# A hybrid state-space, attention and expert network on one core: the time-step projection computed with its weights stationary beside the first chunk, and the soft-plus chain cut into pieces

## The chip, the core and the metric

The kernel runs on one core of a Trainium2 chip. The engines are TensorE (PE), VectorE (DVE), ScalarE (ACT), GpSimd (POOL) and SyncE (SP), and 16 DMA engines move data. Each engine runs its own list of instructions in order and waits on semaphores. The metric is the time of one execution in device microseconds, as a median of several runs. All data is float32 unless marked otherwise. In the traces a float32 matmul appears as two records.

## What is computed

Two layers over 256 latent tokens and 256 context tokens, 512 in all, of width 1024. Layer 0 mixes tokens with a bidirectional state-space scan (SSD), layer 1 with local attention; each is followed by a mixture of 16 experts. Every part starts with a normalisation whose scale and shift come from a conditioning vector c through a large matrix ada_w. The change touches the start of layer 0:

```python
sh1, sc1, g1, sh2, sc2, g2 = split(silu(c) @ ada_w[l] + ada_b[l])
a_l = modulate(rmsnorm(h, norm1_w[l]), sh1, sc1)        # x * (1 + scale) + shift

def project(h):                                          # in ssd_mixer
    zxbcdt = h @ in_w
    z = zxbcdt[..., :D_INNER]
    xbc = silu(centred_dwconv(zxbcdt[..., D_INNER:D_INNER + CONV_DIM], conv_w, conv_b))
    dt_raw = zxbcdt[..., D_INNER + CONV_DIM:]            # 64 columns: 32 heads, two directions
    dt_f = softplus(dt_raw[..., :SSM_HEADS] + dt_bias[0])
    dt_b = softplus(dt_raw[..., SSM_HEADS:] + dt_bias[1])
    return z, xs, bm, cm, dt_f, dt_b

cum = cumsum(dt_c * a_neg, axis=2)                       # in ssd_chunked_scan, per block of 128 tokens
```

## The kernel before

Tokens lie along the columns: hT holds x and aT the normalised input, each as 8 tiles of 128 features by 512 tokens (k from 0 to 7). The order of work is written out by hand for each engine, and semaphores tie the engines together. The opening of the kernel runs like this.

**Loads.** SP issues the DMAs: a slice of constants, x, ctx, erev, nine small loads of packed parameters (packs), then the weight units in the order of the list `order`: ada0 to ada7 (1 MB each, a piece of ada_w), xbc0 (1 MB, two chunks of ssd_in_w as 1024 packets of 1 KB), ada8, ada9, xbc1, and so on. A unit whose slot holds an earlier unit waits until PE is done with that one. ACT issues on its own queue, at the very start: wdtw (the 64 columns of ssd_in_w that give dt_raw, 128x8x64), the router's weights rw, and five rows broadcast over all partitions (dtb, expa, dskip, rb, sink). After the first modulations ACT also issues the rest of the constants, c32 and c16.

**Turning x and the squares.** PE turns x (L1106), with the packed parameters in front of the last piece (L1102). DVE and ACT copy the pieces to hT. ACT squares each tile into aT (L786). PE computes four ada units (L1117: four 32-column tiles of 512 columns each, summed in one bank), then the mean square as eight 512-column matmuls over the squares (L1136), then ada4 to ada7, and turns the resulting rows (ada_turn, L1130).

**Normalisation.** ACT takes the square root (L788), DVE the reciprocal (L1864), then DVE multiplies the eight tiles (L1869); before tile 3 it copies the ada rows (L1832), and before tile 6 it forms shift and scale (L1838, L1846). ACT modulates each tile in two halves (L795).

**Time-step projection.** For each tile k, four matmuls with 128 tokens of aT as stationary weights and the 64 columns of wdtw[k] as moving operand (L1161), so that tokens come out on the partitions. Then a chain on DVE (L1876 to L1894) with one Exp on ACT (L812) computes the soft-plus as a series, dt, and dt times the decay rate (sp[6]).

**Chunks.** in_chunk(i) is eight matmuls of 512 columns (L1174). ACT copies the result with padding (conv_in, L832), DVE convolves in five steps (L1931, L1934), ACT takes Tanh (L839), DVE finishes the SiLU (L1945). Each of the first 14 chunks is followed on PE by one ada unit. After chunk 6 PE forms cumulative sums from sp[6] with triangular matrices (L1291 to L1294). From chunk 14 on, chunks alternate with the scan itself. Later come the gate z, the output projection, the experts (L1491, L1530), attention and the second set of experts, with weights streamed through a ring of slots by SP.

`link` on DVE makes an instruction wait for the one before it. `add_squares(i, k, n)` already existed for the later normalisations: it adds the squares of tile k to ssq. `mean_square_of_sum` multiplies ssq and the last tile's squares with the constant matrix mean.

## Time and profile before

| what | value |
|---|---|
| median of 3 runs | 1526.36 us (1525.91 to 1527.06) |
| the profiled execution | 1528.73 us, of which the span of the trace is 1526.9 us |
| PE busy | 1404.9 us (92%), weight loads 795.6 us |
| DVE busy | 543.7 us (36%) |
| ACT busy | 393.5 us (26%) |
| POOL busy | 152.1 us (10%) |
| mean granted PE clock | 0.968 of full speed |
| DMA | 334.46 MB, mean 219 GB/s |
| chain of waits that ended last | PE 70%, issue on SP 13%, DMA 6%, DVE 5%, ACT 2% |

The span runs from the first to the last instruction; some 1.8 us lie outside it. A share of busy time is an average over stages with different limits, so what a change in one stage is worth is read from that stage. Line numbers in the rows are those of the kernel before.

### The profile page before, as it was taken

To read this page: it belongs to the slowest core of one execution; us is meant where nothing else is said; L and a number is where in the kernel's file an instruction comes from. 1 tells how busy PE (TensorE), PEld (TensorE's weight loads), DVE (VectorE), ACT (ScalarE), POOL (GpSimd) and SP (SyncE) were. 2 spreads that over 40 slices of the span, in tenths; PEclk is the share of its full clock that TensorE was granted. 3 is DMA by queue.
4 is the path that set the end of the run, shared out by engine and by line. 5 is a ranking of instruction groups with operands and counts; after the bars stand their busy time and mean duration, and the time that the engine had idled before them with its cause. 6 is when DMAs were issued, how large, how long until landed. Compare 5 with 4: busy or idle time off the path is not lost.

```text
span 1526.9 us, 28680 instructions
## 1 busy us (share of the span) xinstructions
PE 1404.9 (92%) x12237; PEld 795.6 (52%) x12237; DVE 543.7 (36%) x1010; ACT 393.5 (26%) x961; POOL 152.1 (10%) x181
## 2 busy tenths in 40 slices
PE   5899899999988999989999999998999999989876
PEld 2534444454544444455566555646856775555432
DVE  2445656555553221144122221124254442221112
ACT  2321333334434310040222222204053302221111
POOL 0000113122042200000011111000000001111100
PEclk9799999999999999999999999999999999999988
DMA  9365333344341452152999999993330359999993
GB/s 354 112 216 174 131 111 135 117 138 164 110 138 57 110 138 83 57 195 74 364 356 389 392 382 381 360 362 105 112 111 2 127 195 392 394 392 400 398 404 133
DMA packets 131493, 334.46 MB, mean 219 GB/s; under 512 B 13283, under 2 KB 63259, under 8 KB 125211
## 3 DMA queue, kind: packets, MB, share of 16 engines
q1 hardware_dynamic: 118763, 307.56, 55.2%
q0 software_dynamic: 6208, 12.60, 2.4%
q10 hardware_dynamic: 6384, 12.36, 2.2%
q8 instruction: 100, 1.64, 0.4%
q14 instruction: 38, 0.31, 0.1%
HBM read 325.79 MB, written 14.81 MB: 223 GB/s over the span
## 4 chain that ended last, share of the span: by engine, by line
PE 70%; SPq 13%; DMA 6%; DVE 5%; ACT 2%; issue 2%; DVEq 0%; ACTq 0%; POOLq 0%
PE ps L1174 11%; PE ps L1491 10%; SPq L557 10%; PE ps L1387 7%; PE ps L1191 7%; PE ps L1530 5%; PE ps L1441 5%; SPq L559 3%; PE ps L1117 3%; PE ps L1791 2%; PE ps L1555 2%; PE ps L1703 2%; PE ps L1266 2%; DMA ring<-in_moe_w_down 1%; PE ps L1279 1%
## 5 line engine op out<-in xcount | busy, mean ns | idle before, releaser
L1174 PE MATMUL ps<-aT,ring 128*128 128x512 f32 x384 | 174.6, 604 | 0.0
L1491 PE MATMUL ps<-ring,ssb 128*32 128x256 f32 x2256 | 132.2, 386 | 13.3 <-DMA ring<-in_moe_w_up 12.6
L1491 PE MATMUL ps<-tmp,ssb 128*32 128x256 f32 x1984 | 113.0, 380 | 10.0 <-DMA tmp<-in_moe_w_up 10.0
L2214 DVE COPY big<-ps 32x256 f32<-32x256 f32 x162 | 68.6, 424 | 146.0 <-PE ps L1530 144.3
L1174 PEld LDWEIGHTS ps<-aT,ring 128*128 128x128 f32 x384 | 71.4, 193 | 82.8 <-issue 82.8
L1191 PE MATMUL ps<-aT,ring 128*128 128x512 f32 x256 | 114.2, 595 | 0.0
L2205 DVE TENSOR_TENSOR ssb<-ssb,ps 128x128 f32<-128x128 f32 (+1 forms) x56 | 19.4, 348 | 257.4 <-ACT ssb L968 257.4
L1387 PE MATMUL ps<-big,ring 128*128 128x512 f32 x256 | 110.2, 592 | 0.0
L1491 PEld LDWEIGHTS ps<-ring,ssb 128*32 128x32 f32 x2256 | 74.0, 111 | 65.9 <-DMA ring<-in_moe_w_up 19.7
L1530 PE MATMUL ps<-ring,ssb 128*32 128x256 f32 x1648 | 96.8, 387 | 3.5 <-DMA ring<-in_moe_w_down 2.9
L871 ACT ACTIVATE ssb<-ps,dt 128x128 f32<-128x128 f32 x256 | 73.3, 372 | 88.5 <-PE ps L1254 87.7
L981 ACT COPY big<-ps 32x256 f32<-32x256 f32 x162 | 58.7, 362 | 141.4 <-PE ps L1530 139.9
L1491 PEld LDWEIGHTS ps<-tmp,ssb 128*32 128x32 f32 x1984 | 66.6, 110 | 53.1 <-DMA tmp<-in_moe_w_up 9.5
L1441 PE MATMUL ps<-aT,ring 128*128 128x256 f32 (+1 forms) x288 | 89.3, 468 | 4.4 <-ACT aT L795 4.4
L968 ACT ACTIVATE ssb<-ps 128x128 f32<-128x128 f32 (+1 forms) x56 | 18.2, 325 | 257.3 <-PE ps L1491 257.2
L1387 PEld LDWEIGHTS ps<-big,ring 128*128 128x128 f32 x256 | 48.6, 190 | 61.2 <-issue 61.0
L1191 PEld LDWEIGHTS ps<-aT,ring 128*128 128x128 f32 x256 | 47.2, 190 | 52.6 <-issue 52.6
L1934 DVE SCALAR_TENSOR_TENSOR ring<-ring,par 128x512 f32<-128x512 f32 x96 | 72.2, 752 | 3.4
L1441 PEld LDWEIGHTS ps<-aT,ring 128*128 128x128 f32 x288 | 55.0, 196 | 35.2 <-issue 29.3
L1530 PEld LDWEIGHTS ps<-ring,ssb 128*32 128x32 f32 x1648 | 52.8, 111 | 38.7 <-issue 5.2
L746 POOL DMA_INDIRECT y_rows<-big,sidx x32 | 30.1, 940 | 315.7 <-DVE big L2214 314.3
L786 ACT ACTIVATE aT<-hT 128x512 f32<-128x512 f32 (+1 forms) x32 | 17.7, 574 | 159.8 <-DVE hT L2076 88.5
(393 smaller groups left out, 1828.6 us busy)
## 6 DMA issues: line engine op xcount, KB each, us to landing
ring<-in_ada_w SPq DMA_DIRECT2D x44, 1024.0 KB, 4.9
ring<-in_moe_w_down SPq DMA_DIRECT2D x40, 1024.0 KB, 17.9
ring<-in_moe_w_gate SPq DMA_DIRECT2D x56, 512.0 KB, 11.6
ring<-in_moe_w_up SPq DMA_DIRECT2D x56, 512.0 KB, 15.7
tmp<-in_moe_w_gate SPq DMA_DIRECT2D x48, 512.0 KB, 12.9
tmp<-in_moe_w_up SPq DMA_DIRECT2D x48, 512.0 KB, 16.4
ring<-in_ssd_in_w SPq DMA_DIRECT2D x20, 1024.0 KB, 7.4
tmp<-in_moe_w_down SPq DMA_DIRECT2D x16, 1024.0 KB, 17.6
```

What stands on the lines that cost most here:

```text
L557: sp_.dma_start(pair_slot(u)[:, :, r, :], src).then_inc(s_w[u.slot], 16)
L559: sp_.dma_start(slot(u, 2), down[(j - 4) * 2 * P:(j - 3) * 2 * P, :].rearrange("(k p) n -> p k n", p=P))\
L871: ins = act.activation(E[:, d * HG + h, :], ps[:, 5, j * P:(j + 1) * P], ACT.Exp, bias=dt[:, t, col:col + 1])
L981: ins = act.copy(Y[s % 2][32 * g:32 * g + 32, 256 * c:256 * c + 256], tiled_y[32 * c:32 * c + 32, 2 * h + i, :])
L1174: ins = pe.matmul(ps[:, bank, :], slot(u)[:, k, (i % 2) * P:(i % 2 + 1) * P], aT[:, k, :], start=(k == 0), stop=(k == KD - 1))
L1191: ins = pe.matmul(ps[:, z_bank(i), :], slot(u)[:, k, (i % 2) * P:(i % 2 + 1) * P], aT[:, k, :], start=(k == 0), stop=(k == KD - 1))
L1387: ins = pe.matmul(ps[:, 4 + m % 4, :], w[:, k, :], xT[:, k, :], start=(k == 0), stop=(k == KI - 1))
L1441: ins = pe.matmul(ps[:, 2 * (f % 2) + r, per * h:per * h + per], pair_slot(unit(e, k // 2))[:, k % 2, r, f * P:(f + 1) * P], aT[:, k, per ...
L1491: ins = pe.matmul(tiled_gu[32 * c:32 * c + 32, 2 * h + i, :].rearrange("p (r n) -> p r n", r=2), XgT[l][:, k * C + 32 * g:k * C + 32 * g + ...
L1530: ins = pe.matmul(tiled_y[32 * c:32 * c + 32, 2 * h + i, :], hiddenT[l][:, g, 32 * k:32 * k + 32], slot(units["x", l, s, 4 + k // 2][0], 2 ...
L1934: ins = dve.scalar_tensor_tensor(out=o, in0=pre[i % 2][:, :, tap:tap + S], scalar=par[:, tap * NCONV + ch:tap * NCONV + ch + 1], in1=o, op ...
L2214: ins = dve.tensor_copy(Y[s % 2][32 * g:32 * g + 32, 256 * c:256 * c + 256], tiled_y[32 * c:32 * c + 32, 2 * h + i, :])
```

## The change

1. **Mean square.** DVE adds the squares of tiles 0 to 6 into ssq as ACT produces them (add_squares for k = 1 to 6). PE computes five ada units, then two matmuls, over ssq and over the last tile's squares, in place of eight, then three more ada units. The shared counter s_ssq starts one higher for later users. In the normalisation the ada rows are copied before tile 4 and not 3, shift and scale are formed before tile 7 and not 6.
2. **Projection.** wdtw[k] (128x64) is now stationary and aT[k] (512 columns) moves. Even k write partitions 0 to 63 of PSUM bank 4, odd k partitions 64 to 127. PE takes tiles in pairs: the first chunk's two matmuls for k and k + 1, then the two projection matmuls (dt_parts). DVE copies the bank to dtT. After chunk 1 and its ada unit, PE multiplies the four token blocks of dtT with `two` (two identities on top of each other), which adds the two halves and puts tokens on partitions (dt_sums). POOL builds `two`.
3. **Soft-plus.** The DVE chain is cut into four pieces, which run behind the convolutions and SiLUs of chunks 1 to 4. ACT's Exp, the exponential of the decay rates and the copies of dskip move behind the first Tanh and the second conv_in; its Ln moves from chunk 4 to 5.
4. **Loads.** All loads are issued by SP. Ada0 stands before the packed parameters; behind xbc0 follow wdtw and the rows dtb, expa and dskip; behind ada8, ada9 and xbc1 follow c32, c16 and erev; rw, rb and sink come after four more units. ACT begins with a Silu of one element.

```diff
-        n_consts, n_x, n_bc = 10, 3, 5
+        n_consts, n_late, n_x, n_bc, n_rt = 9, 3, 3, 4, 3
...
-            sp_.dma_start(erev[:, :], a["erev"]).then_inc(s_const, 16)
...
-            for name, v in order:
+            load(*order[0])
+            for i, r, src in packed:
+                sp_.dma_start(packs[r:r + src.shape[0], i, :], src).then_inc(s_const, 16)
+            for name, v in order[1:KD + 1]:
                 load(name, v)
+            sp_.dma_start(wdtw, a["ssd_in_w"][0][:, DI + NCONV * P:DI + NCONV * P + 64].rearrange("(k p) n -> p k n", p=P))\
+                .then_inc(s_bc, 16)
+            for dst, src in ((dtb[:, :], a["ssd_dt_bias"].rearrange("l d h -> (l d h)")),
+                             (expa[:, :], a["ssd_a_log"].rearrange("l d h -> (l d h)")),
+                             (dskip[:, :], a["ssd_d"].rearrange("l h -> (l h)"))):
+                sp_.dma_start(dst, src.partition_broadcast(P)).then_inc(s_bc, 16)
+            for name, v in order[KD + 1:KD + 4]:
+                load(name, v)
...
+            pool.wait_ge(s_x, 16 * n_x)
+            pool.tensor_tensor(two, ident[:, 0:HP], ident[:, HP:P], ALU.add).then_inc(s_set, 1)
...
+            act.activation(small[:, 14:15], small[:, 15:16], ACT.Silu)
...
+                if i == 1:
+                    act.wait_ge(s_sp, 5)
+                    act.activation(sp[1], sp[1], ACT.Exp, scale=-1.0).then_inc(s_sp, 1)
+                    act.wait_ge(s_bc, 16 * n_bc)
+                    act.activation(expa[:, :], expa[:, :], ACT.Exp).then_inc(s_sp, 1)
...
-            for n in range(4):
+            for n in range(5):
                 ada_unit(n)
-            mean_square(0, T, 7)
-            for n in range(4, KD):
+            mean_square_of_sum(0, T, 7, 1)
+            for n in range(5, KD):
                 ada_unit(n)
             ada_turn(0)
-
-
-            pe.wait_ge(s_bc, 16 * 7)
-            for k in range(KD):
-                pe.wait_ge(s_a, k + 1)
-                for t in range(NT):
-                    ins = pe.matmul(ps[:, 4, t * 64:(t + 1) * 64], aT[:, k, t * P:(t + 1) * P], wdtw[:, k, :],
-                                    start=(k == 0 and t == 0), stop=(k == KD - 1), skip_group_check=True)
-            ins.then_inc(s_sp, 1)
...
+            def dt_parts(k):
+                for r in range(k, k + 2):
+                    ins = pe.matmul(ps[HP * (r % 2):HP * (r % 2) + HP, 4, :], wdtw[:, r, :], aT[:, r, :],
+                                    start=(r < 2), stop=(r >= KD - 2))
+                return ins
+
+            def dt_sums():
+                pe.wait_ge(s_sp, 2)
+                pe.wait_ge(s_set, 10)
+                for t in range(NT):
+                    ins = pe.matmul(ps[:, 6, t * 64:(t + 1) * 64], dtT[:, t * P:(t + 1) * P], two, start=True, stop=True)
+                ins.then_inc(s_sp, 1)
+
+            pe.wait_ge(s_bc, 16 * n_bc)
+            for k in range(0, KD, 2):
+                for r in range(k, k + 2):
+                    pe.wait_ge(s_a, r + 1)
+                    in_chunk(0, r, r + 1)
+                ins = dt_parts(k)
+            ins.then_inc(s_sp, 1)
...
             for i in range(AHEAD):
-                in_chunk(i)
+                if i:
+                    in_chunk(i)
                 ada_unit(KD + i)
+                if i == 1:
+                    dt_sums()
...
-            norm(0, T, {3: ada_rows, 6: modulation})
+            for k in range(1, KD - 1):
+                add_squares(0, k, T)
+            norm(0, T, {4: ada_rows, 7: modulation})
...
+                if 1 <= i <= 4:
+                    softplus(i - 1)
```

PE, from the first ada unit on. In these names ring, ssb and tmp are the slots that hold weight units, cs is the conditioning vector, aT the squares and later the input, and ssb in the projection is wdtw. Before:

```order
L1117 MATMUL ps<-ring,cs 32x512 x16
L1136 MATMUL ps<-aT,mean 128x512 x8
L1117 MATMUL ps<-ssb,cs 32x512 x8
L1117 MATMUL ps<-tmp,cs 32x512 x8
L1130 MATMUL ps<-c,ring 128x128 x4
L1161 MATMUL ps<-ssb,aT 128x64 x32
L1174 MATMUL ps<-aT,ring 128x512 x8
L1117 MATMUL ps<-ring,cs 32x512 x4
L1174 MATMUL ps<-aT,ring 128x512 x8
L1117 MATMUL ps<-ring,cs 32x512 x4
```

Now, the same place:

```order
L1128 MATMUL ps<-ring,cs 32x512 x16
L1128 MATMUL ps<-ssb,cs 32x512 x4
L1152 MATMUL ps<-ssq,mean 128x512
L1154 MATMUL ps<-aT,mean 128x512
L1128 MATMUL ps<-ssb,cs 32x512 x4
L1128 MATMUL ps<-tmp,cs 32x512 x8
L1141 MATMUL ps<-c,ring 128x128 x4
L1176 MATMUL ps<-aT,ring 128x512 x2
L1287 MATMUL ps<-aT,ssb 64x512 x2
```

Five ada units stand ahead of a mean square of two matmuls, and the projection has gone into the first chunk in pairs of 64-wide matmuls; the last two rows come four times in all. A little further on, from the last pair to chunk 2, PE now has:

```order
L1287 MATMUL ps<-aT,ssb 64x512 x2
L1128 MATMUL ps<-ring,cs 32x512 x4
L1176 MATMUL ps<-aT,ring 128x512 x8
L1128 MATMUL ps<-ring,cs 32x512 x4
L1295 MATMUL ps<-ncum,ssb 128x64 x4
L1176 MATMUL ps<-aT,ring 128x512 x8
```

The four 64-column matmuls over ssb (dtT) and ncum (`two`) stand between chunk 1's ada unit and chunk 2.

SP's loads, before, from ada4 on (ring<-in_ssd_in_w 128x8x256 is an xbc unit):

```order
L535 DMA ssb<-in_ada_w 128x2048 x2
L535 DMA tmp<-in_ada_w 128x2048 x2
L535 DMA ring<-in_ssd_in_w 128x8x256
L535 DMA ring<-in_ada_w 128x2048 x2
L535 DMA ring<-in_ssd_in_w 128x8x256
L535 DMA ring<-in_ada_w 128x2048 x2
```

Now, the same place:

```order
L533 DMA tmp<-in_ada_w 128x2048 x2
L533 DMA ring<-in_ssd_in_w 128x8x256
L637 DMA ssb<-in_ssd_in_w 128x8x64
L642 DMA dtb<-in_ssd_dt_bias 128x64
L642 DMA expa<-in_ssd_a_log 128x64
L642 DMA dskip<-in_ssd_d 128x32
L533 DMA ring<-in_ada_w 128x2048 x2
L533 DMA ring<-in_ssd_in_w 128x8x256
L645 DMA c<-in_c 128x896
```

The load of wdtw (ssb) and three rows have come between xbc0 and ada8, and c32 (c), c16 (big) and erev behind xbc1.

## Rows read from the trace of the kernel before

**Rows 1.** Busy time by stretches; columns: us, engines, PEclk, DMA share, GB/s.
```profile
0.00:44.00 44.00, 23.96 (x124) 11.66 (x124) 12.70 (x19) 13.30 (x22) 1.01 (x13) 0.92 0.92 351
...
66.00:240.00 174.00, 164.69 (x684) 75.04 (x677) 101.22 (x153) 51.41 (x118) 11.21 (x10) 0.97 0.45 152
```
**Rows 2.** Timeline of PE; start us, length us, line, operation, what ended idle time.
```profile
9.73 4.83 PE L1106 MATMUL ps<-c,big 128*128 128x128 f32 x28 [9.73 <-DMA big<-in_ctx]
...
20.82 1.06 PE L1117 MATMUL ps<-ring,cs 128*32 128x512 f32 x8 [1.41 <-DMA ring<-in_ada_w]
...
23.30 1.93 PE L1117 MATMUL ps<-ring,cs 128*32 128x512 f32 x8 [1.41 <-DMA ring<-in_ada_w]
...
25.16 7.84 PE L1136 MATMUL ps<-aT,mean 128*128 128x512 f32 x16
...
39.77 0.69 PE L1130 MATMUL ps<-c,ring 128*128 128x128 f32 x4 [3.20 <-DVE ring L1832]
...
43.10 13.88 PE L1161 MATMUL ps<-ssb,aT 128*128 128x64 f32 x64 [2.64 <-ACT aT L795]
...
56.78 9.06 PE L1174 MATMUL ps<-aT,ring 128*128 128x512 f32 x16
...
65.77 1.07 PE L1117 MATMUL ps<-ring,cs 128*32 128x512 f32 x8
...
66.76 7.13 PE L1174 MATMUL ps<-aT,ring 128*128 128x512 f32 x16
```
**Rows 3.** Busy time by stretches, around the falls of PE's clock.
```profile
23.30:26.70 3.40, 3.40 (x10) 1.03 (x11) 0.00 (x0) 0.00 (x0) 0.00 (x0) 0.51 1.01 422
...
43.10:57.00 13.90, 13.90 (x65) 13.90 (x66) 0.00 (x0) 8.02 (x15) 1.39 (x1) 0.50 0.25 94
...
57.00:60.40 3.40, 3.40 (x5) 1.33 (x6) 2.72 (x5) 0.87 (x4) 0.00 (x0) 0.50 0.00 0
```
**Rows 4.** Timeline of DVE.
```profile
33.83 3.35 DVE L1864 RECIPROCAL rstd<-rstd 128x512 f32<-128x512 f32 x1 [17.68 <-ACT rstd L788]
...
37.22 1.90 DVE L1869 TENSOR_TENSOR aT<-hT,rstd 128x512 f32<-128x512 f32 x3
...
62.15 3.19 DVE L1888 SCALAR_TENSOR_TENSOR ssb<-ssb 128x256 f32<-128x256 f32 x7
...
82.62 0.55 DVE L1931 TENSOR_SCALAR ring<-ring,par 128x512 f32<-128x512 f32 x1 [3.76 <-ACT ring L832]
```
**Rows 5.** Timeline of ACT.
```profile
16.91 4.26 ACT L786 ACTIVATE aT<-hT 128x512 f32<-128x512 f32 x8
...
41.87 2.56 ACT L795 ACTIVATE aT<-aT,mod,amod 128x256 f32<-128x256 f32 x5 [8.14 <-DVE amod L1846]
```
**Rows 6.** Stretch from 10 to 11 us, and ACT's DMA queue in the first 20.
```profile
10.00:11.00 1.00, 1.00 (x6) 1.00 (x6) 0.12 (x1) 0.00 (x0) 0.00 (x0) 1.00 0.33 57
...
q10 hardware_dynamic: 2800, 0.43, 12.7%
```
**Rows 7.** Issues on SP's and ACT's queues; of the last two, median us to landing.
```profile
18.34 0.38 SPq L535 DMA_DIRECT2D ring<-in_ssd_in_w  x1
...
21.95 7.53 SPq L535 DMA_DIRECT2D ring<-in_ada_w  x1
...
3.02 1.10 ACTq L771 DMA_DIRECT2D expa<-in_ssd_a_log  x1
...
dtb<-in_ssd_dt_bias ACTq DMA_DIRECT2D x1, 32.0 KB, 10.0
...
c<-in_c SPq DMA_DIRECT2D x1, 64.0 KB, 2.0
```
**Rows 8.** Timeline of PE, small matmuls at full clock.
```profile
115.12 0.41 PE L1291 MATMUL ps<-ssb,c 128*128 128x32 f32 x2
...
229.68 1.09 PE L1279 MATMUL ps<-ssb 128*64 128x128 f32 x16 [0.60 <-issue]
```
**Rows 9.** Waits of SP's DMA issues: us in total, times, longest.
```profile
SPq L535 <- PE ps L1117: 380.9, 40, 36.1
```

More of the change, by code:

```diff
@@ L302, in build @@
         four = ncum[:, 0, 0:NE]
+        two = ncum[:, 0, :]
         ps = ctx.enter_context(nc.psum_tensor("ps", [P, 8, 512], F32))
@@ L526, in _ @@
                       (2, 48, a["c_ctx"].rearrange("(c p) -> c p", p=P))]
-            for i, r, src in packed:
-                sp_.dma_start(packs[r:r + src.shape[0], i, :], src).then_inc(s_const, 16)
             held = {}
@@ L632, in moe @@
                     after(l, following, False)
-            for name, v in order:
+            load(*order[0])
[10 more added lines that the diff above has]
+            for name, v in order[KD + 1:KD + 4]:
+                load(name, v)
+            sp_.dma_start(c32[:, P:], a["c32"][:, P:]).then_inc(s_const, 16)
+            sp_.dma_start(c16f, a["c16"]).then_inc(s_const, 16)
+            sp_.dma_start(erev[:, :], a["erev"]).then_inc(s_const, 16)
+            for name, v in order[KD + 4:2 * KD]:
+                load(name, v)
+            sp_.dma_start(rw[:, :, :], a["router_w"].rearrange("(k p) n -> p k n", p=P)).then_inc(s_bc, 16)
+            for dst, src in ((rb[:, :], a["router_bias"]), (sink[:, :], a["attn_sink"].rearrange("l h -> (l h)"))):
+                sp_.dma_start(dst, src.partition_broadcast(P)).then_inc(s_bc, 16)
+            for name, v in order[2 * KD:]:
                 load(name, v)
@@ L762, in _ @@
         def _(act):
-            act.dma_start(wdtw, a["ssd_in_w"][0][:, DI + NCONV * P:DI + NCONV * P + 64].rearrange("(k p) n -> p k n", p=P))\
-                .then_inc(s_bc, 16)
-            act.dma_start(rw[:, :, :], a["router_w"].rearrange("(k p) n -> p k n", p=P)).then_inc(s_bc, 16)
-            rows = [(dtb[:, :], a["ssd_dt_bias"].rearrange("l d h -> (l d h)")),
-                    (expa[:, :], a["ssd_a_log"].rearrange("l d h -> (l d h)")),
-                    (dskip[:, :], a["ssd_d"].rearrange("l h -> (l h)")),
-                    (rb[:, :], a["router_bias"]), (sink[:, :], a["attn_sink"].rearrange("l h -> (l h)"))]
-            for dst, src in rows:
-                act.dma_start(dst, src.partition_broadcast(P)).then_inc(s_bc, 16)
             act.wait_ge(s_set, 4)
+            act.activation(small[:, 14:15], small[:, 15:16], ACT.Silu)
             for k in range(1, KD, 2):
@@ L797, in norm_modulate @@
                         ins.then_inc(s_a, 1)
-                if i == 0:
-                    act.dma_start(c32[:, P:], a["c32"][:, P:]).then_inc(s_const, 16)
-                    act.dma_start(c16f, a["c16"]).then_inc(s_const, 16)
             def ready0(k):
@@ L808, in _ @@
             norm_modulate(0, 0, T, 7, ready0)
-            act.wait_ge(s_sp, 3)
-            act.activation(sp[1], sp[1], ACT.Exp, scale=-1.0).then_inc(s_sp, 1)
-            act.wait_ge(s_bc, 16 * 7)
-            act.activation(expa[:, :], expa[:, :], ACT.Exp).then_inc(s_sp, 1)
-            for w in range(2):
-                act.copy(dcol[w * HP:(w + 1) * HP, :].unsqueeze(2),
-                         dskip[w * HP:(w + 1) * HP, :].rearrange("p (k w) -> p k w", w=2)[:, :, w:w + 1]).then_inc(s_dcol, 1)
             def decays():
@@ L908, in _ @@
                 conv_in(i)
-                if i == 4:
-                    act.wait_ge(s_sp, 6)
+                if i == 1:
[3 more added lines that the diff above has]
+                    act.activation(expa[:, :], expa[:, :], ACT.Exp).then_inc(s_sp, 1)
+                    for w in range(2):
+                        act.copy(dcol[w * HP:(w + 1) * HP, :].unsqueeze(2),
+                                 dskip[w * HP:(w + 1) * HP, :].rearrange("p (k w) -> p k w", w=2)[:, :, w:w + 1]).then_inc(s_dcol, 1)
+                if i == 5:
+                    act.wait_ge(s_sp, 8)
                     act.activation(lnd, dt[:, :, :].rearrange("p t n -> p (t n)"), ACT.Ln).then_inc(s_ln, 1)
@@ L1307, in _ @@
                     turn_x(i - 2)
[L1309 removed]
+            pe.wait_ge(s_set, 11)
             pe.wait_ge(s_cT, 3)
@@ L1869, in norm @@
                         dve.tensor_tensor(aT[:, k, part], hT[:, k, part], rstd[:, part], ALU.mult).then_inc(s_nx, 1)
[L1871 to L1874 removed]
+            for k in range(1, KD - 1):
+                add_squares(0, k, T)
+            norm(0, T, {4: ada_rows, 7: modulation})
+            dve.wait_ge(s_bc, 16 * n_bc)
             dve.wait_ge(s_sp, 1)
[L1876 to L1877 removed]
```

89 lines of the change are left out of this document (50 added, 39 removed).

## The prediction, made before the change was run

> **What bounds the kernel now.** I read the table by stretches first. After the opening 44 us, TensorE (PE) is busy 164.69 of the next 174 us, so from there on PE's own work sets the pace; in the opening 44 us it is busy only 24 [rows 1]. The opening is therefore where time can come out, and what comes out ahead of the long PE run moves all that stands behind it.
>
> PE's timeline of that opening gives the chain [rows 2]. It waits for x and ctx (9.73), turns x, waits 1.41 us each for the weight units ada2 (20.82) and ada3 (23.30), sums squares from 25.16, waits for ada_rows (39.77), waits for the first modulated tile (43.10), computes the time-step projection in 13.88 us, and starts the first chunk at 56.78; the next ada unit starts at 65.77. Between the sum of squares and 43.10 the chain runs through ScalarE (ACT) and VectorE (DVE): Sqrt when the sum is done at 33.0, reciprocal of 3.35 us at 33.83, norm products of 0.63 each, modulation from 41.87 [rows 4, 5].
>
> The granted clock is the third view. It was 0.51 from 23.3 to 26.7, after the two waits for weights; 0.50 throughout the projection, after PE had been idle around ada_turn; still 0.50 in the first 3.4 us of the chunk; then it rose [rows 3]. So the projection ran wholly at the lower level (1.2 GHz) and did not lift it, while chunk matmuls of 512 columns did.
>
> **Sum of squares (removes eight matmuls from the chain).** Before: from 25.16 for 7.84 us, to 33.0, and ada4 stood behind it [rows 2]. Now DVE adds the squares and PE needs two matmuls. When can these start? ACT's squares begin at 16.91 and take 0.53 each [rows 5]; DVE's six adds, each at the 0.63 us of a 512-column product [rows 4] and some 0.1 of waiting for the one before, start after the second square and end 4.4 us later, near 22.4. The loads can come earlier: all that the ACT queue carried, 2800 small packets, had used 12.7% of 20 us, 2.5 us of all engines, in competition with x [rows 6]; this leaves the front, and so does erev. Also ada0 is now in line directly behind ctx, where the rate had fallen to 57 GB/s after 10 us [rows 6]. I put x 1.6 us earlier, so the adds end at 20.8; the units gain the 2.5 us and one more from the hole, 3.5 in all. Units land 2.48 us apart (20.82, 23.30), so ada4, now ahead of the mean square, would have landed at 25.8 and lands at 22.3. That is later than the adds, and sets the start. Warm prices: a unit of four 32-column tiles 0.99 (65.77 to 66.76), a 512-column matmul 7.1/8 = 0.89 [rows 2]. Work 0.99 + 2 x 0.89 = 2.8; at half clock for 3.4 us, as before, 1.7 of it is done, the other 1.1 follow: end at 22.3 + 3.4 + 1.1 = 26.8, **6.2 us earlier** than 33.0. Bounds: warm and ada4 at 21.5 gives 24.3; ada4 gaining only 1.5 us gives 28.8.
>
> The preloaded Silu table takes two table loads out of ACT's start, but ada4's landing, not ACT's squares, sets the mean square in this sum: nothing, and up to the 1.3 us of a load if that landing should come sooner.
>
> **The norm chain.** Reciprocal and products are as before, but four products instead of three stand ahead of ada_rows and seven instead of six ahead of the modulation: one product more, 0.63 [rows 4]. So the first modulation moves from 41.87 to 41.87 - 6.2 + 0.6 = 36.3; ada5 to ada7 (the last lands at 33.2 - 3.5 = 29.7) are done before ada_rows is wanted at 33.5. PE's first input, 1.2 us after that, is there at 37.5 instead of 43.10, **5.6 us earlier**.
>
> **Parameter loads past the projection's start.** wdtw and three broadcast rows now sit on SP's queue behind the 1024-packet xbc0. Before, the issue right behind xbc0 (18.34) took 7.53 us, until 29.48 [rows 7]. Taking 3.5 us off, SP is free for wdtw at 26; wdtw has as many packets as xbc0, so the first row waits again, until xbc0 is nearly in, near 31.5 (29.7 for ada7 plus 2.5, less a little). Three rows at 1.10 each [rows 7] make 34.8, and with the 2.0 us that a small load took to land on a queue still empty [rows 7] they land at 36.8: just ahead of 37.5. I take it as hidden, with no more than a microsecond to spare. Xbc0 itself (32.2) is in time. Units ada8 and on are issued behind the rows at 35, and not wanted before 50. The later loads (c32, c16, erev, router rows) are six more issues, 0.4 to 1.1 us each, on an engine that spends 380.9 us waiting for PE [rows 9]: nothing.
>
> **Projection and first chunk.** Removed: 13.88 us at half clock, 32 matmuls of 0.434, thus 0.217 warm and 6.9 in all. Its weight loads were busy 13.9 of 13.9 us [rows 3], so each 128x128 load of aT cost as much as its 64 columns. Added: eight matmuls of 512 columns in four pairs on separate column halves. No row shows such a pair at 512 columns. If the two overlap fully it is 0.89, if not at all 1.78. Nearest: eight 64-wide matmuls of 128 columns took 1.09 [rows 8], 0.27 a pair, where columns alone make 0.22 for one and 0.44 for two; and four 32-wide ones took 0.99 for 0.89. I take 0.97, so 3.9 for four pairs. Chunk plus pairs: 7.1 + 3.9 = 11.0 warm. From 37.5 with the clock low for 3.4 us as in [rows 3]: 1.7 done, 9.3 left, end 37.5 + 3.4 + 9.3 = **50.2 instead of 65.77**, 15.6 us earlier. ACT's modulations take 1.0 a tile (two halves of 0.51) and end near 44.5, ahead of a half-clock PE.
>
> What the row shows first: 32 matmuls of 64 columns filled 13.88 us, and their weight loads filled it too. The Trainium skill, TensorEngine Tiling (Array Packing), Performance Considerations, says that a matmul of one column costs what one of 60 does, so that 64 columns would be paid by columns. By columns alone the old projection streams 32 x 64 = 2048 of them, as much as four pairs of 512, 7.1 us at half clock; whoever costed it so would take 6.8 us less for this change and arrive at 1518.5. The measured row decides against that.
>
> Added on PE as well: dt_sums, four matmuls of 64 columns with 128x128 weights. Bounds: the old ones at 0.217, the first of the triangular matmuls (32 columns, two records) at 0.41 with its end [rows 8]; so 0.9 to 1.6, and I take 0.9, since the old ones have this very shape. **Net: 15.6 - 0.9 = 14.7.**
>
> **Soft-plus in pieces.** Off PE's path before, too: the chain ran beside the chunk. In each 8.06 us of chunk and ada unit DVE was idle 3.76 [rows 4]. The largest piece, part 2, is seven steps of 3.19 and one of 0.3: it fits. The first piece, 1.2, comes behind conv(1) and silu(0), and ACT's Exp waits for it, with conv_tanh(1) queued behind; silu(1) comes two chunks before its buffer is wanted. The cumulative sums want the result after chunk 6, some 20 us later. Nothing. Were DVE's idle time not there, the four pieces would cost their own length, some 9 us. DVE's copy of the products (0.6) has chunk 1 to hide in, ahead of dt_sums; POOL's new add of two slices of the identity runs after x has come, when POOL does nothing else, and its cast of c16 is wanted only behind 160 us.
>
> **To the end.** SP's loads wait for PE's own progress, 380.9 us in 40 waits on PE's ada units [rows 9], so the streams shift with it. The profiled span of 1526.9 becomes 1512.2; the profiled run's 1528.7 becomes 1514.0; against the median of 1526.4: **1511.7 us**.
>
> **Rivals.**
> - *The clock stays low through the mixed chunk,* as it did through the projection. Against: chunk matmuls lifted it in 3.4 us. Then 22.0 us from 37.5 end at 59.5; gain 6.3 - 0.9 = 5.4: 1521. Chance 0.06.
> - *The rows hold the projection up by some microseconds.* At four more, 1516; at seven, 1519. Chance 0.12.
> - *Given back later:* PE waits for DVE and ACT around 180 to 240 us, or a differently falling clock, eat what came in. Nothing in that stretch is tied to absolute time, but each fall of the clock is worth some 2 us (the first chunk's 9.06 against 7.1); six such would be needed. 1524 to 1529. Chance 0.07.
> - *Slower, by one queue.* If each of the small loads blocks as ada8's did: wdtw to 26, then 7.5 each for dtb, expa and dskip, 48.5, and they land, as dtb did on the busy queue [rows 7], 10 us later, 58.5. Then chunk and pairs end at 58.5 + 12.7 = 71.2, plus 0.9: 6.3 us slower, 1532.7. It decides once rows land after 52.2 (64.9 less 12.7). The Trainium skill, DMA: Bandwidth & Descriptors, Queues, rings and completion order, has each issuing engine's transfers consumed in order of its own ring, so the small ones would stand behind the big ones; the 7.53 us row agrees with that much. For it also: the margin is thin. Against: after xbc0 nothing large is left in line. Chance 0.05.
> - *The change does not reach its aim:* ada4 is late, so the mean square gains only 3; all else as told: 1515. Within the forecast.
> - *The forecast,* with the clock up all along (rows in at 36.8, + 11.0 = 47.8; gain 17.1: 1509) to half-overlapped pairs (1.4 lost), a late ada4 (2.0) and a clock low twice as long (1.7), gain 9.6: 1517. Chance 0.70.
>
> **How the numbers follow.** Low end: 1507, the warm case with rows and units 2 us earlier. High end: 1519, which takes in most of the second rival, with the first, the give-back and the slower case outside. A difference under 0.2% (3 us) can't be told from none. Faster: 0.70 + 0.06 + 0.12 = 0.88; within 0.2%: 0.07; slower: 0.05.
>
> **What would show it.** Right: Sqrt near 27, first modulation near 36, PE's chunk beginning within 1 us of it, pairs of about 1.0, ada8's matmuls near 50 and a PE without a gap to about 162. Wrong: a PE waiting for loads of dtb, expa or dskip; a clock of 0.5 past 41; pairs of 1.8; a gap in front of dt_sums or chunk 2; gaps growing behind 160 us.

## The result, and the profile of the changed kernel

The changed kernel took 1507.65 us (median of 4 runs, 1505.93 to 1509.72) against 1526.13 (4 runs, 1523.32 to 1527.06) of the kernel before on the same chip: ratio 0.9877, interval 0.9852 to 0.9902. It is faster by 18.5 us; forecast were 14.7 us and 1511.7. Its profiled execution took 1509.05 us with a span of 1507.2, where that of before has 1526.9. One execution of the kernel before, of 3655.65 us, is left out of every mean and ratio here.

PE's timeline of the changed kernel's opening, to be held against [rows 2] (start us, length us, line, operation, xrecords, in brackets the idle time before and what ended it):

```profile
22.49 1.06 PE L1128 MATMUL ps<-ssb,cs 128*32 128x512 f32 x8 [1.42 <-DMA ssb<-in_ada_w]
23.48 1.12 PE L1152 MATMUL ps<-ssq,mean 128*128 128x512 f32 x2
24.44 1.02 PE L1154 MATMUL ps<-aT,mean 128*128 128x512 f32 x2
...
31.58 1.94 PE L1128 MATMUL ps<-tmp,cs 128*32 128x512 f32 x8 [3.07 <-DMA tmp<-in_ada_w]
34.33 1.11 PE L1141 MATMUL ps<-c,ring 128*128 128x128 f32 x4 [0.81 <-DVE ring L1858]
37.72 3.44 PE L1176 MATMUL ps<-aT,ring 128*128 128x512 f32 x4 [2.27 <-DMA dskip<-in_ssd_d]
41.09 1.08 PE L1287 MATMUL ps<-aT,ssb 128*64 128x512 f32 x4
42.10 1.98 PE L1176 MATMUL ps<-aT,ring 128*128 128x512 f32 x4
...
50.87 1.07 PE L1128 MATMUL ps<-ring,cs 128*32 128x512 f32 x8
...
59.93 1.10 PE L1295 MATMUL ps<-ncum,ssb 128*128 128x64 f32 x8
```

The mean square is done at 25.4, not 33.0. The projection has no stretch of its own: PE begins the first chunk at 37.72 (before: the projection at 43.10, the chunk at 56.78), and ada8, 65.77 in [rows 2], comes at 50.87, 14.9 us earlier. The four 64-column matmuls of dt_sums take 0.94 of that. Chunk 2 begins 13.95 us earlier.

Granted clock and busy time by stretches (us, PE, PEld, DVE, ACT, POOL, PEclk, DMA share, GB/s), the answer to [rows 1] and [rows 3]:

```profile
22.00:31.00 9.00, 5.04 (x28) 1.15 (x28) 4.98 (x5) 0.91 (x2) 0.00 (x0) 0.97 1.01 401
31.00:40.00 9.00, 5.33 (x15) 2.08 (x16) 4.48 (x9) 3.57 (x8) 0.00 (x0) 0.50 0.73 256
...
41.00:44.00 3.00, 3.00 (x9) 0.88 (x8) 0.00 (x0) 3.00 (x7) 0.00 (x0) 1.00 1.07 370
```

The clock was up during the mean square, fell shortly before 31 while PE waited for ada7, stayed at 0.50 (1.2 GHz) while PE waited for the norm, and was up again by 41, some 3 us after the chunk's matmuls had begun.

DVE and ACT, for [rows 4] and [rows 5]:

```profile
21.55 0.69 DVE L1883 TENSOR_TENSOR ssq<-ssq,aT 128x512 f32<-128x512 f32 x1
...
33.59 0.69 DVE L1858 COPY ring<-ps 128x512 f32<-128x512 f32 x1 [1.48 <-PE ps L1128]
...
36.43 7.97 ACT L808 ACTIVATE aT<-aT,mod,amod 128x256 f32<-128x256 f32 x16 [10.23 <-DVE amod L1872]
```

DVE's last add of squares ends at 22.2, just ahead of ada4's landing. Later DVE waits 1.48 us for PE's product of ada7, which no row of the kernel before shows.

SP's issues, for [rows 7]:

```profile
18.51 8.19 SPq L637 DMA_DIRECT2D ssb<-in_ssd_in_w  x1
26.74 4.71 SPq L642 DMA_DIRECT2D dtb<-in_ssd_dt_bias  x1
31.49 0.43 SPq L642 DMA_DIRECT2D expa<-in_ssd_a_log  x1
31.96 0.43 SPq L642 DMA_DIRECT2D dskip<-in_ssd_d  x1
```

And the chain of waits that ended last, in the opening (start us, us, what):

```profile
18.51 8.19 SPq L637
...
26.74 4.71 SPq L642
...
31.96 5.71 DMA dskip<-in_ssd_d
...
37.72 3.44 PE ps L1176 x4
```

So the last thing the first chunk waited for was the row dskip, landed at 37.67. The prediction had it 0.7 us ahead of the norm. It was level with it: PE can begin 1.19 to 1.24 us after the first modulation starts (36.00 and 37.19 in e11, 41.87 and 43.10 before), and here that started at 36.43.

### The profile page after: what moved, and what is told of

It reads as the page before. It is cut to its first block, busy times and chain, and to the rows that moved or that the text cites. A ratio compares the mean times of both kernels' runs of the same rounds, so it can differ in the third digit from the quotient of the medians.

```text
span 1507.2 us, 28592 instructions
## 1 busy us (share of the span) xinstructions
PE 1389.9 (92%) x12185; PEld 790.8 (52%) x12185; DVE 547.4 (36%) x1017; ACT 392.1 (26%) x961; POOL 152.4 (10%) x182
## 4 chain that ended last, share of the span: by engine, by line
PE 68%; SPq 16%; DMA 6%; DVE 5%; issue 3%; ACT 2%; DVEq 0%; ACTq 0%; POOLq 0%
SPq L555 11%; PE ps L1176 11%; PE ps L1517 9%; PE ps L1413 7%; PE ps L1193 7%; PE ps L1467 5%; PE ps L1556 5%; SPq L557 3%; PE ps L1128 3%; DMA tmp<-in_moe_w_down 3%; PE ps L1817 2%; PE ps L1581 2%; PE ps L1729 2%; PE ps L1268 2%; PE ps L1281 1%
## 5 line engine op out<-in xcount | busy, mean ns | idle before, releaser
L1517 PE MATMUL ps<-ring,ssb 128*32 128x256 f32 x2256 | 136.8, 386 | 10.7 <-DMA ring<-in_moe_w_up 10.0
L1517 PE MATMUL ps<-tmp,ssb 128*32 128x256 f32 x1984 | 116.1, 381 | 6.4 <-DMA tmp<-in_moe_w_up 6.3
L1517 PEld LDWEIGHTS ps<-ring,ssb 128*32 128x32 f32 x2256 | 87.9, 111 | 53.8 <-DMA ring<-in_moe_w_up 15.8
L1556 PE MATMUL ps<-ring,ssb 128*32 128x256 f32 x1648 | 96.5, 386 | 2.3 <-DMA ring<-in_moe_w_down 1.7
L1556 PEld LDWEIGHTS ps<-ring,ssb 128*32 128x32 f32 x1648 | 52.1, 111 | 37.9 <-DMA ring<-in_moe_w_down 3.6
L1517 PE MATMUL ps<-ssb 128*32 128x256 f32 x944 | 57.0, 387 | 1.4 <-DMA ssb<-in_moe_w_up 0.7
```

Of the source, the lines that this page charges most:

```text
L1517: ins = pe.matmul(tiled_gu[32 * c:32 * c + 32, 2 * h + i, :].rearrange("p (r n) -> p r n", r=2), XgT[l][:, k * C + 32 * g:k * C + 32 * g + ...
L1556: ins = pe.matmul(tiled_y[32 * c:32 * c + 32, 2 * h + i, :], hiddenT[l][:, g, 32 * k:32 * k + 32], slot(units["x", l, s, 4 + k // 2][0], 2 ...
```

## Experiments

The theory: the whole gain is made ahead of chunk 2, out of three parts (squares, projection, loads), and is passed on one to one. Rivals: that one part carries nearly all; that the rows' queue holds the start up by microseconds; that the pieces of the soft-plus, or the clock, make something behind the opening.

One table first, since each experiment below draws on it. "Opening": how much earlier than in the first trace of before the same instructions of DVE, ACT and SP start around 180 us, where the shift is the same for all of them. "Whole": (1 - ratio) times 1526 us, from the timed runs. Each opening is read from one trace.

| kernel | opening | ratio (interval) | whole |
|---|---|---|---|
| changed | 14.0 | 0.9877 (0.9852 to 0.9902) | 18.8 |
| e1 squares only | 2.7 | 0.9997 (0.9978 to 1.0017) | 0.5 |
| e2 projection only | 10.8 | 0.9925 (0.989 to 0.996) | 11.4 |
| e3 loads only | 4.8 | 0.9951 (0.992 to 0.9983) | 7.5 |
| e4 all but the loads | 10.4 | 0.9945 (0.9914 to 0.9976) | 8.4 |
| e5 changed, again | 13.6 | 0.990 (0.9873 to 0.9928) | 15.3 |
| e6 changed, PE's waits filled | 15.7 | 0.990 (0.9871 to 0.9929) | 15.3 |
| e7 changed, 4.1 us of delay | 10.6 | 0.9935 (0.9914 to 0.9955) | 9.9 |
| e8 changed, soft-plus in one | 12.8 | one run, 1509.01 us | |
| e9 before, again | 0.9 | 0.9999 (0.9976 to 1.0023) | 0.2 |
| e10 filled, rows first | 16.4 | 0.9898 (0.9866 to 0.993) | 15.6 |
| e11 rows first | 14.4 | one run, 1504.69 us | |
| e12 rows first, timed | 13.9 | 0.9911 (0.9882 to 0.994) | 13.6 |

**e1, the squares alone.** In the kernel before, DVE adds the squares and PE does two matmuls for the mean; loads and projection stay.

```diff
-            for n in range(4):
+            for n in range(5):
                 ada_unit(n)
-            mean_square(0, T, 7)
-            for n in range(4, KD):
+            mean_square_of_sum(0, T, 7, 1)
+            for n in range(5, KD):
```

> The kernel before with the first part alone: squares summed on VectorE, two matmuls for the mean square, five ada units ahead of it; loads and projection as before. If the parts add up as the prediction summed them: ada4 lands near 25.8 as before, the mean square ends at 28.6 (clock up) to 30.3 (clock down) and not 33.0, one norm product more; every later event 2.1 to 3.8 us earlier, so 1522 to 1524. Rival, that the early landing of the units is what pays and this part gives nothing without it: under 1 us.

```profile
25.79 1.06 PE L1117 MATMUL ps<-ssb,cs 128*32 128x512 f32 x8 [1.42 <-DMA ssb<-in_ada_w]
...
34.23 1.92 PE L1117 MATMUL ps<-tmp,cs 128*32 128x512 f32 x8 [2.39 <-DMA tmp<-in_ada_w]
...
40.28 13.89 PE L1161 MATMUL ps<-ssb,aT 128*128 128x64 f32 x64 [2.22 <-ACT aT L795]
```

PE's timeline of e1: ada4 lands at 25.79 and sets the mean square (done at 28.7, 4.3 us earlier). Only 2.8 of that reach the projection (40.28 for 43.10): 0.6 is the one norm product more that now stands ahead, and 0.8 is DVE's wait for PE's product of ada7, which landed at 34.23. The opening came as expected. The median did not: the 0.5 us of the whole, with its interval of -2.6 to 3.4, can be told neither from nothing nor from 2.7.

**e2, the projection alone.** The kernel before with the pairs, dt_sums, and the soft-plus chain behind them.

```diff
-            for k in range(KD):
-                pe.wait_ge(s_a, k + 1)
-                for t in range(NT):
-                    ins = pe.matmul(ps[:, 4, t * 64:(t + 1) * 64], aT[:, k, t * P:(t + 1) * P], wdtw[:, k, :],
...
+            for k in range(0, KD, 2):
+                for r in range(k, k + 2):
+                    pe.wait_ge(s_a, r + 1)
+                    in_chunk(0, r, r + 1)
+                ins = dt_parts(k)
```

> The kernel before with the projection beside the first chunk and the soft-plus in pieces; squares and loads as before. Start stays near 43.1; chunk with pairs takes 12.7 us (clock down for the first 3.4) and not 22.7, dt_sums add 1.0: everything behind is 9 us earlier, 1517. Rival, that the clock stays down through the mixed chunk: 22 us, no gain, 1526.

```profile
40.70 3.69 PE L1168 MATMUL ps<-aT,ring 128*128 128x512 f32 x4 [2.17 <-issue]
44.32 1.08 PE L1279 MATMUL ps<-aT,ssb 128*64 128x512 f32 x4
...
54.10 1.07 PE L1120 MATMUL ps<-ring,cs 128*32 128x512 f32 x8
```

From the first product to ada8 it takes 13.4 us where before took 22.67: 9.3 less, 8.3 after dt_sums. The other 2.4 of the opening's 10.8 are not the edit's: in this execution the mean square began earlier (23.51 for 25.16) and ended earlier (30.6 for 33.0), at full clock (eight matmuls in 7.13 for 7.84). The kernel before itself made half of that in e9, below, where its projection began at 41.89. The Trainium skill, TensorEngine Tiling (Array Packing), Performance Considerations, says that a matmul of one column takes as long as one of 60; whoever prices 64 columns by their number on that ground would expect 6.8 us less of this edit. The 8.3 us net and 1.01 a pair speak against that where each such matmul loads 128x128 float32 weights. A row of the kernel before points the same way, its 32-column matmuls with 128x128 weights at full clock:

```profile
115.59 0.39 PE L1291 MATMUL ps<-ssb,c 128*128 128x32 f32 x2
115.81 0.39 PE L1292 MATMUL ps<-ssb,c 128*128 128x32 f32 x2
```

They start 0.22 us apart, nearly what the 64-column ones cost at full clock (0.94 for the four of dt_sums), although they have half the columns.

**e3, the loads alone.** The kernel before with SP and ACT issuing as in the changed one: wdtw, dtb, expa and dskip on SP behind xbc0, erev behind xbc1.

```diff
-            act.dma_start(wdtw, a["ssd_in_w"][0][:, DI + NCONV * P:DI + NCONV * P + 64].rearrange("(k p) n -> p k n", p=P))\
...
-            sp_.dma_start(erev[:, :], a["erev"]).then_inc(s_const, 16)
...
+            for name, v in order[1:KD + 1]:
+                load(name, v)
+            sp_.dma_start(wdtw, a["ssd_in_w"][0][:, DI + NCONV * P:DI + NCONV * P + 64].rearrange("(k p) n -> p k n", p=P))\
...
+            sp_.dma_start(erev[:, :], a["erev"]).then_inc(s_const, 16)
```

> The kernel before with all loads issued by SP in the new order; squares by matmul, projection as before. If the new order alone makes the units land 3.3 us earlier, the mean square starts that much earlier and all behind it is some 3 us earlier: 1523. Rival, that the parameter rows behind xbc0 hold the projection (they landed at 37.7 in the changed kernel): here the projection starts at 40 or later anyway, so no loss from them. If the DMA engines rather than the order set the landing: 0 to 1 us.

```profile
21.08 7.13 PE L1141 MATMUL ps<-aT,mean 128*128 128x512 f32 x16
...
38.32 13.89 PE L1166 MATMUL ps<-ssb,aT 128*128 128x64 f32 x64 [2.62 <-ACT aT L803]
```

PE's timeline of e3: the mean square begins at 21.08 for 25.16, since x and the units land earlier (ada3 at 20.08 for 23.30), and it takes 7.13 at full clock. The projection begins at 38.32, 4.8 earlier. wdtw and the rows did not hold it: SP was done with dskip at 32.4, as in the changed kernel.

**e4, all but the loads.** The complement: squares, projection and soft-plus as changed, loads as before.

> The changed kernel with the loads issued as in the kernel before. The clear sum of e1 and e2: 11 to 13 us earlier than before, 1513 to 1515, thus 1 to 3 us short of the 14.0 us that the changed kernel has gained by 66 us. Rival, that the new order of loads pays nothing or costs: 14 us or more.

```profile
26.28 1.06 PE L1123 MATMUL ps<-ssb,cs 128*32 128x512 f32 x8 [1.42 <-DMA ssb<-in_ada_w]
...
40.20 3.75 PE L1171 MATMUL ps<-aT,ring 128*128 128x512 f32 x4 [2.17 <-ACT aT L800]
```

Without the early loads ada4 lands at 26.28 instead of 22.49, the chunk begins at 40.20 instead of 37.72, and the opening gives 10.4 instead of 14.0, less than the 11 to 13 us expected. So the loads are worth 3.6 us inside the change, where e3 alone gave 4.8; 2.5 of the 3.6 is the earlier start, and 1.1 is the clock, which rose later here (chunk and pairs took 14.3 us for 13.2). Squares 2.7, projection 8.3 and loads 3.6 make 14.6 against the 14.0 seen. No part carries the change alone, and the projection is over half.

**e5, the changed kernel once more,** as the partner of e6 to e8 on their chip.

> The changed kernel again, timed closer. Up to chunk 1 its trace stands 14.0 us ahead of the kernel before; the medians of four runs differ by 18.5. If the further 4.5 us is where the clock's falls happened to lie in these executions, more runs bring the difference back to 12 to 16 us and the shift behind 180 us differs in this trace from the -16.8 and -19.5 of the first. If it is a lasting gain of the scan or of the experts, the difference stays at 17 us or more and the later shifts repeat.

Start of the chunk 37.71, again ended by dskip; ada8 51.31. The opening repeats within 0.4 us. The whole, 15.3 us, is in the 12 to 16 us by which the surplus would be scatter. Behind the opening the two traces of the same kernel drift apart by up to 2.9 us (at 240 us), but at their ends they stand 19.7 and 19.2 us ahead of the first trace of before: this pair alone does not show the surplus of the first comparison to be scatter.

**e6, PE's waits in the opening filled.** The added products are read by nobody.

```diff
+            def keep_warm(n):
+                for _ in range(n):
+                    pe.matmul(ps[:, 5, :], mean[:, :], ssq[:, :], start=True, stop=True)
+
-            for n in range(5, KD):
-                ada_unit(n)
+            ada_unit(5)
+            keep_warm(1)
+            ada_unit(6)
+            keep_warm(3)
+            ada_unit(7)
+            keep_warm(1)
             ada_turn(0)
+            keep_warm(2)
```

> The changed kernel with seven more matmuls of 512 columns into an unused PSUM bank, which nothing reads: one behind ada5, three behind ada6, one behind ada7, two behind ada_turn. If idle PE is what brings the clock down in the opening, it stays up to the first chunk: the first two chunk matmuls take 1.98 and not 3.44 us, ada7's 1.0 and not 1.9; 1.5 to 2.5 us earlier at ada8 than in e5. Rival: the fillers only delay what stands behind them on PE, or the clock falls anyway: no gain, up to 1 us lost.

Stretches of e6 (columns as above) and its first chunk on PE:

```profile
31.00:41.00 10.00, 8.08 (x29) 2.76 (x29) 4.50 (x9) 5.60 (x12) 0.00 (x0) 1.00 0.77 275
```
```profile
37.50 1.98 PE L1185 MATMUL ps<-aT,ring 128*128 128x512 f32 x4 [1.80 <-DMA dskip<-in_ssd_d]
39.42 1.08 PE L1296 MATMUL ps<-aT,ssb 128*64 128x512 f32 x4
...
49.20 1.06 PE L1128 MATMUL ps<-ring,cs 128*32 128x512 f32 x8
```

The clock never fell, and ada8 came at 49.20, 2.1 us ahead of e5: the half-clock stretch does cost its share. It also gives the warm price of the mixed chunk that the prediction had put at 11.0: 49.20 - 37.50 = 11.7. A pair takes 1.01, and the two chunk matmuls (four records) between pairs 1.92 instead of 1.78, so a pair costs 1.16 in all. The whole, 15.3 us, is no better than e5's.

**e7, a delay in the norm.** Nine more products on DVE, whose result isn't used, ahead of the first reciprocal of the changed kernel.

```diff
                 dve.wait_ge(s_rs, rstd_to(i) + 1)
+                if i == 0:
+                    for _ in range(9):
+                        link(dve.tensor_scalar(arow, hT[:, 0, :], 1.0, None, ALU.mult))
```

> The changed kernel with nine linked VectorE products ahead of the reciprocal, whose result is not used: about 5.4 us more on the chain of the opening. If what the opening gains or loses moves the rest one for one, chunk 1 and the end are 5.4 us later than in e5, within the scatter of the runs (2 us). If part of the opening is covered by loads or given back later: 3 us or less.

The first timeline is DVE's, the second PE's:

```profile
26.31 4.12 DVE L1889 TENSOR_SCALAR ring<-hT 128x512 f32<-128x512 f32 x9 [3.61 <-ACT rstd L801]
...
36.26 0.68 DVE L1858 COPY ring<-ps 128x512 f32<-128x512 f32 x1
```
```profile
40.28 3.75 PE L1176 MATMUL ps<-aT,ring 128*128 128x512 f32 x4 [2.17 <-issue]
```

The nine products took 4.1 us, 0.46 each: less than nine products of two tiles (0.6 each, 5.4), by which the delay was chosen. The chunk began 2.57 us later than in e5. The other 1.6 us vanished: DVE's wait for PE's product of ada7 was 1.24 us in e5 (1.48 in the changed kernel's first trace) and is gone here, and e7's mean square ended 0.2 us earlier than e5's. So the norm chain had some 1.3 us of slack: ada7, not the squares, is what is late next. ada8 (54.23) came 2.9 us later than e5's, not the 5.4 expected. The whole fell by 5.4, with intervals that overlap, so the runs can't tell whether more than the 2.9 was passed on.

**e8, the soft-plus in one piece** behind the second convolution.

```diff
-                if 1 <= i <= 4:
-                    softplus(i - 1)
+                if i == 1:
+                    for part in range(4):
+                        softplus(part)
```

> The changed kernel with all four pieces of the soft-plus chain behind conv(1), 9.6 us in a row on VectorE. By the prediction the pieces lie off PE's path either way as long as PE stays two chunks behind what VectorE has done: no gap on PE, chunk 2 to 13 at the same times as in e5. Rival: conv(2) and conv_in(3) come late enough that PE waits in front of chunk 4 or 5, some 1 to 6 us.

DVE's timeline of e8, then PE's:

```profile
65.06 0.41 DVE L1908 TENSOR_TENSOR ssb<-ps,dtb 128x256 f32<-128x256 f32 x1
...
74.58 0.42 DVE L1929 SCALAR_TENSOR_TENSOR ssb<-dt,expa 128x256 f32<-128x256 f32 x1
74.92 0.54 DVE L1966 TENSOR_SCALAR ring<-ring,par 128x512 f32<-128x512 f32 x1
...
79.78 0.55 DVE L1966 TENSOR_SCALAR ring<-ring,par 128x512 f32<-128x512 f32 x1 [0.58 <-ACT ring L833]
```
```profile
69.07 1.06 PE L1128 MATMUL ps<-ring,cs 128*32 128x512 f32 x8
70.07 7.13 PE L1176 MATMUL ps<-aT,ring 128*128 128x512 f32 x16
```

The chain holds DVE from 65.06 to 75.0 and pushes the convolution of chunk 2 behind it; by 79.78 DVE is waiting for ACT again, and PE has no gap. PE was busy 110.00 of the 110 us from 53 to 163. The opening of this execution was 1.2 us slower than the changed kernel's first trace, but ada8 was already at 52.06 (clock up later), ahead of the soft-plus. The pieces are worth nothing here, as the prediction had them.

**e9, the kernel before once more.**

> The kernel before once more, for a second trace of its own. By theory A (the 3 to 4 us of the difference that lie behind the opening are where the clock happens to fall in one execution, in code that both kernels share) this trace differs from the first of before by 1 to 5 us in stretches behind 180 us, while its opening is within 1.5 us of the first one's (the eighth ada unit lands within 1.5 us of 65.77). By theory B (the change itself saves 3 us behind the opening) this trace follows the first of before within 1 us in every stretch up to 740 us.

Stretches of the first trace of before, then nearly the same work in e9:

```profile
410.00:450.00 40.00, 36.17 (x215) 18.76 (x207) 20.32 (x27) 16.11 (x45) 16.06 (x12) 0.96 0.39 132
```
```profile
406.00:446.00 40.00, 35.89 (x216) 18.45 (x208) 21.67 (x29) 16.18 (x45) 16.04 (x12) 1.00 0.39 132
```

Theory A held. The opening of e9 is 0.9 us ahead of the first trace, but by 450 us it is 5.4 ahead, at 740 4.0, at the end 4.7: the same program. Of this, 1.5 us fall into the stretch shown, with the clock at 0.96 in one execution and 1.00 in the other over nearly the same work. So the shift of 19.7 us at the end of the two first traces is not 19.7 us of the change.

**e10 and e11, the rows first.** The loads of wdtw, dtb, expa and dskip stand ahead of xbc0 instead of behind it (in the list, order[KD]); e10 also has e6's filling.

```diff
-            for name, v in order[1:KD + 1]:
+            for name, v in order[1:KD]:
                 load(name, v)
             sp_.dma_start(wdtw, a["ssd_in_w"][0][:, DI + NCONV * P:DI + NCONV * P + 64].rearrange("(k p) n -> p k n", p=P))\
...
+            load(*order[KD])
```

> The changed kernel with both: PE's waits in the opening filled with products that nobody reads (7 of 512 columns), and the time-step projection's weights and the three parameter rows issued by SP ahead of the fourth x slice of the context. In e6 the projection's first product began at 37.50, with the row dskip as the last thing waited for; with the rows landed early it waits for the first piece of aT alone. If the rows were the end of that wait: start at 36.9 to 37.3 and 1 to 2.5 us earlier than the changed kernel as a whole. Rival: the two loads of weights (wdtw) take the place of xbc0 and ada7 in the queues, and ada7, which already landed last of the units, comes later still: start at 37.5 or later, no gain.

> The changed kernel with the rows and wdtw issued ahead of the fourth x slice and nothing else. If the rows end the wait ahead of the chunk by 0.3 us: start at 37.4 in place of 37.7, and no product of the chunk waits for a row. The prediction took the rows as hidden; this tells by how much they were not. Rival: as above, ada7 comes later and the start with it.

(The expectations call xbc0 a slice of the context; it is the unit of ssd_in_w described above.) PE's timeline of e11, then its chain of waits:

```profile
31.16 1.94 PE L1129 MATMUL ps<-tmp,cs 128*32 128x512 f32 x8 [2.73 <-DMA tmp<-in_ada_w]
...
37.19 3.60 PE L1177 MATMUL ps<-aT,ring 128*128 128x512 f32 x4 [2.17 <-ACT aT L809]
```
```profile
9.37 21.74 DMA tmp<-in_ada_w
...
31.16 1.98 PE ps L1129 x8
...
36.00 1.10 ACT aT L809 x2
...
37.19 3.60 PE ps L1177 x4
```

With the rows in, the start moved from 37.72 to 37.19 and the chain went over to ada7: its transfer, PE's product, ada_rows, the modulation. e10's start was 36.73 and its opening 16.4, the earliest of all, a little better than expected; the gain of 1 to 2.5 us in the whole that was expected with it is not there (15.6). The rival, by which ada7 comes later still, fell: PE began on it at 31.16 in e11 and at 31.57 in e10. But of e11's 0.5 us, 0.4 is ada7, which came at 31.16 for 31.58; e12, the same kernel, has ada7 at 31.54 and starts at 37.57. So the rows cost the change itself some 0.1 us, and two chains end within that tenth. They cost 0.8 us once PE is filled (37.50 in e6, 36.73 in e10), when ada7's product takes 1.06 us instead of 1.94 and the norm is done sooner.

**e12, e11 again with times.**

> The kernel of e11 again, now with times. Theory A (behind the opening two traces of one kernel differ by some us by where the clock falls): its own median is within 1 us of 1509, since the opening gives 0.4 us over the changed kernel, and this trace's shifts behind 180 us are not those of e11 (by 1 us or more in a stretch). Theory B (moving the rows saves some 4 us, as the one time of e11, 1504.69, says): median at 1504 to 1506, and the shift of the end against before again near 24 us.

Median 1510.83 (6 runs, 1508.06 to 1513.04), start 37.57, and the shift of the end 20.7 instead of e11's 24.0. A's own figure, within 1 us of 1509, is missed by 0.8, B's 1504 to 1506 by 5: the 1504.69 of e11 was one execution. No variant beat the changed kernel by more than the runs scatter, though e6 and e10 have an opening 1.7 to 2.4 us shorter in their traces.

## Why the prediction was right, and where it was not

**The sum of squares: right, its clock not.** ada4 landed at 22.49 (forecast 22.3) and set the start. The mean square ended at 25.4, not 26.8, because the clock did not fall behind the waits for weights; the lower bound of 24.3 was the warm case. This differs from execution to execution: in e8, the same program up to there, the clock was at 0.81 from 22 to 31 and the mean square ended at 27.1, near the forecast. DVE's adds were mis-sized and it did not show: x came 0.9 us earlier, not 1.6, and the adds ended at 22.2, not 20.8, still 1.2 us before PE wanted their sum at 23.5. e1 and e4 show that without the loads this part gives 2.8 and 2.9 us at the start of what follows, not the 4 us by which its own end moves.

**The norm chain: the right sum of two wrong terms.** First modulation 36.43 (forecast 36.3). The step said that ada5 to ada7 were done before ada_rows was wanted: it failed. Units came 2.5 us apart up to ada4, but PE began on ada7 at 31.58 instead of 29.7, its product took 1.94 us at the lower clock, and DVE waited 1.48 us for it. That took back the 1.4 us which the clock had given, so the sum came out by luck; in e8, where the mean square was late, DVE did not wait, and the first modulation came at 36.54 all the same. The spacing of 2.48 us up to ada7 did not hold with the old loads either: e1 has ada7 at 34.23, not 33.2. Why it comes late was not tested apart. e7 measured the slack, e11's chain shows ada7 at its head.

**The rows: hidden, by wrong numbers and with nothing to spare.** Forecast: SP free for wdtw at 26, blocked at the first row to 31.5, three rows of 1.10, landing 2.0 after issue, 36.8. Measured: wdtw's issue held SP for 8.19 and dtb's for 4.71, to 31.45, as forecast; expa and dskip took 0.43 each, so the issues ended 2.4 us earlier than I had it. But dskip landed 5.7 us after its issue began, not 2.0, at 37.7. That is 0.9 us later than forecast, while the norm came 0.1 us later, so the two stood level and the row cost some 0.1 us; with PE filled it cost 0.8 (e6 against e10). The rival in which rows hold the projection by four or seven microseconds did not come, nor did the queue that blocks 7.5 us for every row: behind the blocked one, small loads went at once.

**Projection and chunk: right, one term too small.** The stretch at half clock was as said (3.0 us of the chunk for 3.4). The term mis-sized is the warm price: 11.7 in e6, not 11.0. The pair's own 1.01 was near the 0.97 taken; what was missed are 0.14 us around each pair, in the 128-wide matmuls next to it. So ada8 came at 50.87 for 50.2: 0.7 from this term, 0.2 from the start, less 0.2 for the shorter stretch at half clock. dt_sums took 0.94 for 0.9. Net at chunk 2: 13.95 us, forecast 14.7.

**Soft-plus, Silu table, later loads: nothing, as said.** e8 shows it for the pieces; the Silu table and the later loads were not run apart. PE is gapless from 53 to 163 us even with the chain in one piece.

**To the end: one to one on average; the surplus in the first comparison is probably not the change's.** The first result was 18.5 us for an opening of 14.0. Over the eleven timed kernels of the table, whole minus opening lies between -2.2 and +4.8 us and averages 0.2. The median of 1507.65 lies just above the range's lower end of 1507, and by luck: that end was reckoned for rows and units 2 us earlier, which did not come. Against the runs of before on the same chip, means of the changed kernel give 3.9 us more than its opening in the first comparison and 2.2 more in e5; those of e6, e7, e10 and e12, the same program behind the opening, 0.0 to 0.6 more. Two traces of before differ by 3.8 us behind the opening (e9), two of the changed kernel by up to 2.9 on the way and 0.1 at the end. The places are in code that both share: where the clock falls between 180 and 450 us, and the expert stage, where DMA is busy 0.97 of the time before and 0.93 after:

```profile
765.00:1050.00 285.00, 271.94 (x4151) 161.85 (x4143) 70.28 (x156) 60.93 (x166) 27.37 (x41) 0.99 0.97 361
```
```profile
765.00:1050.00 285.00, 275.01 (x3959) 177.21 (x3952) 71.97 (x159) 64.49 (x171) 25.39 (x39) 0.99 0.93 344
```

(before, then changed; the same stretch holds work shifted by 16 us.) e11 ran 0.2 to 0.4 us ahead of the changed kernel's trace up to 680 us and 3.7 ahead at 800, with nothing changed there. What stays open: the runs of the changed kernel in both comparisons taken together (10, mean 1509.5) are 16.7 us below those of before on all chips (76, mean 1526.2, standard deviation 3.9), 3 us more than the opening, while by the same means e1, e2 and e4 are below theirs. And the traces hint at the clock: between 75 and 600 us PE stood at 1.2 GHz for 20.5, 20.5 and 13.7 us in before, e1 and e9, and for 6.8 to 17.1, on average 11.1, in the eight traces with the changed kernel's opening or one near it (13.7, 3.4 and 6.8 in e2, e3 and e4). Those 7 us less would be worth some 3.5 us of matmul time, an estimate from these sums. Whether an earlier opening makes a fall of the clock behind 180 us less likely was not settled; no run here sets the time of those falls apart from the kernel.

## What to carry to other kernels

A product with few moving columns and a fresh 128x128 weight load each was priced by its loads here (64 columns 0.43 us at 1.2 GHz, with the loads busy throughout): turn it round, so that the small operand is stationary and the long one streams, and put it where its input is already being streamed; it then cost its columns plus a little for changing over (1.16 us a pair where 512 columns alone take 0.89). When a chain is shortened, list all that end within two microseconds behind it: here a mean square that ended 7.6 us earlier brought the start forward by 5.4, with a weight unit and a row next in line. And before a few microseconds are put down to an edit, take a second trace of the same kernel: compare how far the same instructions have moved just behind the edit, not at the end.

## What was unexpected of the hardware

- An issue on SP's queue behind a transfer of 1024 packets held SP for 8.19 us and the next, of a 128x64 row, for 4.71; the two behind that took 0.43 each. With the rows ahead of xbc0 (e11), wdtw's issue took 0.45 and dtb's 16.02, and PE's start was still not later.
- Four pairs of 64-wide, 512-column matmuls on separate column halves took 1.01 us each and made the 128-wide ones between them 0.14 dearer; alone a matmul of 512 columns takes 0.89.
- Two executions of the kernel before moved 4.5 us apart between 180 and 450 us; 1.5 of it in 40 us of nearly the same work, with the clock at 0.96 in one and 1.00 in the other.
- Keeping PE busy with unused products in the opening held the clock at 1.00 and brought 2.1 us there, but nothing that the medians show.
